# The end of a token mixer in another order: turned heads in the queries' place, the second tile's up products ahead of the first tile's, merging on VectorE, places of their own for the forget units

## What is computed

```python
def token_mixers(h, layer, ...):
    proj = h @ w_in                       # queries, keys, values of 3 branches, forget logits, gate logits
    dq, dk, dv, sq, sk, sv, fq, fk, fv, f_logit, g_logit = split(proj)
    o_diff = diff_attention(rope(dq), rope(dk), dv, lam)        # 4 heads, two score maps each
    o_diff = rms_norm(o_diff, diff_norm_g) * (1.0 - lam_init)
    o_sb = stick_breaking_attention(sq, sk, sv)                 # 4 heads
    o_fox = forgetting_attention(fq, fk, fv, log_sigmoid(f_logit + b_forget))   # scores + F_t - F_s
    gates = sigmoid(g_logit.reshape(B, S, 3, D))
    merged = (gates[:, :, 0] * (o_diff @ w_up_diff)
              + gates[:, :, 1] * (o_sb @ w_up_sb)
              + gates[:, :, 2] * (o_fox @ w_up_fox))
    return merged @ w_out
```

## Time and profile before

| | us |
|---|---|
| median of 3 runs | 1640.66 (1640.36 to 1644.25) |
| the profiled execution, its own time | 1641.09 |
| its span, first to last instruction | 1639.3 |
| TensorE busy | 1543.1 (94%) |
| VectorE busy | 959.9 (59%) |
| ScalarE busy | 743.1 (45%) |
| GpSimd busy | 40.5 (2%) |
| mean granted TensorE clock, 1 is full speed | 0.969 |

### The profile page before, as it was taken

The page is one execution under the profiler, slowest core; times in us unless marked ns, Lnnn a source line. Parts: engine busy times, 40 slices in busy tenths (PEclk is TensorE's granted clock), DMA queues, the critical chain, the costliest instruction groups (busy, mean ns, idle before and its releaser), DMA issues.

```text
span 1639.3 us, 18611 instructions
## 1 busy us (share of the span) xinstructions
PE 1543.1 (94%) x7572; PEld 1138.8 (69%) x7572; DVE 959.9 (59%) x883; ACT 743.1 (45%) x687; POOL 40.5 (2%) x30
## 2 busy tenths in 40 slices
PE   5999988999998998988999999999999999999995
PEld 4977766788886886867888536885368853688632
DVE  5547566555556637656799306993169931699413
ACT  3356653434432446653577205772057720577201
POOL 0000031000000000022000000000000000000000
PEclk9998989999999998988899999999999999999998
DMA  8353244454553352245999999999999999999994
GB/s 313 115 206 116 90 171 148 187 188 180 186 199 129 129 202 107 91 164 201 389 359 370 365 425 425 425 425 424 425 425 425 425 425 425 425 425 425 398 425 186
DMA packets 67013, 473.79 MB, mean 289 GB/s; under 512 B 8064, under 2 KB 8192, under 8 KB 10096
## 3 DMA queue, kind: packets, MB, share of 16 engines
q1 hardware_dynamic: 66096, 467.98, 70.8%
q0 software_dynamic: 832, 4.63, 0.8%
HBM read 471.53 MB, written 1.05 MB: 288 GB/s over the span
## 4 chain that ended last, share of the span: by engine, by line
PE 81%; DVE 10%; ACT 4%; issue 2%; DMA 2%; POOL 1%; SPq 0%; DVEq 0%; ACTq 0%
PE ps L1583 20%; PE ps L1584 19%; PE ps L1585 19%; PE ps L1929 11%; PE ps L1963 5%; PE ps L1889 2%; DVE lo_a L1026 2%; DMA raw_a<-in_w_item 1%; PE ps L1936 1%; ACT w_hi L698 1%; PE ps L1749 1%; PE ps L1613 1%; ACT w_hi L936 1%; DVE lo_b L1369 1%; DMA raw_a<-in_w_mix 1%
## 5 line engine op out<-in xcount | busy, mean ns | idle before, releaser
L1026 DVE TENSOR_TENSOR lo_a<-raw_a,w_hi 128x2048 fp32r<-128x2048 f32 (+2 forms) x117 | 251.2, 2151 | 198.7 <-ACT w_hi L698 197.7
L698 ACT ACTIVATE w_hi<-raw_a 128x2048 fp32r<-128x2048 f32 (+2 forms) x117 | 209.4, 1796 | 179.1 <-PE ps L1585 173.9
L1583 PE MATMUL ps<-w_hi,act_hi 128*128 128x512 f32 (+1 forms) x640 | 255.1, 399 | 26.3 <-DVE act_lo L1092 10.9
L1584 PE MATMUL ps<-lo_a,act_hi 128*128 128x512 f32 (+1 forms) x640 | 250.2, 391 | 0.0
L1585 PE MATMUL ps<-w_hi,act_lo 128*128 128x512 f32 (+1 forms) x640 | 249.8, 390 | 0.0
L1369 DVE TENSOR_TENSOR lo_b<-raw_b,w_hi 128x2048 fp32r<-128x2048 f32 x84 | 191.1, 2288 | 18.4 <-ACT w_hi L936 18.2
L936 ACT ACTIVATE w_hi<-raw_b 128x2048 fp32r<-128x2048 f32 x84 | 161.2, 1924 | 61.5 <-PE ps L1585 61.5
L1583 PE MATMUL ps<-w_hi,x_hi 128*128 128x512 f32 x448 | 176.6, 394 | 5.4 <-DVE lo_b L1369 3.2
L1585 PE MATMUL ps<-w_hi,x_lo 128*128 128x512 f32 x448 | 174.6, 390 | 0.0
L1369 DVE TENSOR_TENSOR lo_a<-raw_a,w_hi 128x2048 fp32r<-128x2048 f32 x71 | 161.5, 2289 | 18.1 <-ACT w_hi L936 17.9
L1583 PEld LDWEIGHTS ps<-w_hi,act_hi 128*128 128x128 f32 x640 | 125.8, 197 | 55.4 <-DVE lo_a L1026 8.4
(11 more groups left out here) (257 smaller groups left out, 2132.7 us busy)
## 6 DMA issues: line engine op xcount, KB each, us to landing
raw_a<-in_w_item SPq DMA_DIRECT2D x189, 1024.0 KB, 12.8
raw_b<-in_w_item SPq DMA_DIRECT2D x168, 1024.0 KB, 17.3
raw_a<-in_w_mix SPq DMA_DIRECT2D x60, 1024.0 KB, 4.8
raw_w<-in_w_item SPq DMA_DIRECT2D x21, 1024.0 KB, 16.4
raw_a<-in_w_mix SPq DMA_DIRECT2D x8, 512.0 KB, 3.5
ln_gb<-in_ln_mix POOLq DMA_DIRECT2D x2, 1024.0 KB, 5.1
cst<-in_consts SPq DMA_DIRECT2D x1, 1206.0 KB, 19.6
h<-in_x SPq DMA_DIRECT2D x2, 512.0 KB, 7.6
```

The source lines that it names most:

```text
L698: nc.scalar.activation(w_hi[:, HI_SLOT[g], 0:n], raw(slot)[:, 0:n], ACT.Copy).then_inc(s_hi, 1)
L1026: nc.vector.tensor_tensor(w_lo(slot)[:, 0:n], raw(slot)[:, 0:n], w_hi[:, HI_SLOT[g], 0:n].bitcast(F32), ALU.subtract).then_inc(s_lo, 1)
L1583: nc.tensor.matmul(dst, xh, wh, start=start, stop=False)
L1584: nc.tensor.matmul(dst, xh, wl, start=False, stop=False)
```

## The change

- `F_PART`, `f_hi`, `w_upper`: the upper halves of the two forget units lie in small places of their own. The ring of four holds only full units, so a unit's predecessor in its place (`HI_BEFORE`) is another one.
- `scores`: two heads' score matmuls one after the other, then their two forget products.
- `gates_copy` ahead of `exps` in the two `sb` groups, on ScalarE.
- The turned heads are split into `hd_hi` and `hd_lo`, in the queries' and keys' place, and the merged columns into `act_hi` and `act_lo`.
- Gate unit (5, 0), heads 3, the transposes of tile 1 and the turned weights of groups 4 and 5 come before gate unit (5, 1); the root mean square of group 3 starts before that unit.
- Column half 0 of the up products goes by tiles: tile 1 of all three branches, then tile 0.
- The third branch is added on VectorE, after the gating of a column half; the lower halves of the merged left columns come after all of column half 1.

```diff
-HEADS_JOB = [(1, 0, 4), (1, 1, 5), (0, 0, 2), (0, 1, 3)]
+HEADS_JOB = [(1, 0, 4), (1, 1, 5), (0, 0, 2), (0, 1, 4)]
...
-HI_SLOT = {_g: _q % HRING if _g < MOE_BASE else (_q - MOE_BASE + MOE_BASE % HRING) % MOE_HRING
-           for _q, _g in enumerate(SPLIT_UNITS)}
-HI_BEFORE = {_g: ([x for x in SPLIT_UNITS[:_q] if HI_SLOT[x] == HI_SLOT[_g]] or [None])[-1]
-             for _q, _g in enumerate(SPLIT_UNITS)}
+F_PART = {_b + U_F + _hk: _hk for _b in MIX_BASE for _hk in range(2)}
+FULL_UNITS = [g for g in SPLIT_UNITS if g not in F_PART]
+FULL_MIX = MOE_BASE - len(F_PART)
+HI_SLOT = {_g: _q % HRING if _g < MOE_BASE else (_q - FULL_MIX + FULL_MIX % HRING) % MOE_HRING
+           for _q, _g in enumerate(FULL_UNITS)}
+HI_BEFORE = {_g: ([x for x in FULL_UNITS[:_q] if HI_SLOT[x] == HI_SLOT[_g]] or [None])[-1]
+             for _q, _g in enumerate(FULL_UNITS)}
+for _g, _hk in F_PART.items():
+    HI_BEFORE[_g] = ([x for x in F_PART if x < _g and F_PART[x] == _hk] or [None])[-1]
...
+        f_hi = place("f_hi", [P, 2, 4 * NF], F32R)
...
-        mrg_hi = at("mrg_hi", [P, KT, SEQ], F32R, qkT_at)
-        mrg_lo = at("mrg_lo", [P, KT, SEQ], F32R, qkT_at + KT * SEQ * 4)
+
+        hd_hi = at("hd_hi", [P, KT, SEQ], F32R, qkT_at)
+        hd_lo = at("hd_lo", [P, KT, SEQ], F32R, qkT_at + KT * SEQ * 4)
...
+        def w_upper(g):
+
+            return f_hi[:, F_PART[g], :] if g in F_PART else w_hi[:, HI_SLOT[g], :]
...
 # GpSimd
                     pool.wait_ge(s_gm, l * 6 + (3 * cc + 2))
                     for t in range(TILES):
                         nc.gpsimd.tensor_tensor(cat[:, t, 512 * cc:512 * cc + 512], part(t, 0), part(t, 1), ALU.add).then_inc(s_pch, 1)
-
-                    pool.wait_ge(s_gm, l * 6 + (3 * cc + 3))
-                    pool.wait_ge(s_pch, l * 4 + (2 * cc + 2))
-                    for t in range(TILES):
-                        m = cat[:, t, 512 * cc:512 * cc + 512]
-                        nc.gpsimd.tensor_tensor(m, m, part(t, 2), ALU.add).then_inc(s_mrg, 1)
...
 # ScalarE, mixer
-                for g in range(1, 6):
+                for g in range(1, 5):
                     exps_first(g)
                     split(nb + U_GATE + 2 * g + 3, words(U_GATE + 2 * g + 3))
                     if g >= 2:
                         heads_copy(g - 2)
-                    exps(g)
-                    gates_copy(g)
+                    if GROUPS[g][0] == "sb":
+                        gates_copy(g)
+                        exps(g)
+                    else:
+                        exps(g)
+                        gates_copy(g)
                     split(nb + U_GATE + 2 * g + 4, words(U_GATE + 2 * g + 4))
                     turned_copy(g - 1)
-                    if g in (2, 5):
+                    if g == 2:
                         root(4)
-                transposed_hi(l * 4 + 1, act_hi, (0, 1), HEADS_JOB)
+
+                split(nb + U_UP + 1, words(U_UP + 1))
+                exps(5)
+                heads_copy(3)
+                transposed_hi(l * 4 + 1, hd_hi, (0, 1), HEADS_JOB)
+                turned_copy(4)
                 turned_copy(5)
+                root(4)
+                split(nb + U_UP + 2, words(U_UP + 2))
+                gates_copy(5)
                 heads_copy(4)
-                transposed_hi(l * 4 + 1, act_hi, (2,), HEADS_JOB)
                 heads_copy(5)
-                transposed_hi(l * 4 + 1, act_hi, (3,), HEADS_JOB)
+                transposed_hi(l * 4 + 1, hd_hi, (2, 3), HEADS_JOB)
                 for cc in range(2):
+                    split(nb + U_UP + 3 + cc, words(U_UP + 3 + cc))
                     for t in range(TILES):
                         part = gates[:, t, :, 512 * cc:512 * cc + 512]
                         nc.scalar.activation(part, part, ACT.Sigmoid).then_inc(s_sg, 1)
 
-                for k in range(U_UP, U_OUT + 2 + ahead):
+                for k in range(U_UP + 2, U_OUT + 2 + ahead):
                     split(nb + k + 3, words(k + 3))
                     if k == U_UP + 4:
-                        transposed_hi(l * 4 + 2, mrg_hi, (0, 1), MERGED_JOB)
+                        transposed_hi(l * 4 + 2, act_hi, (0, 1), MERGED_JOB)
                     if k == U_OUT:
-                        transposed_hi(l * 4 + 2, mrg_hi, (2, 3), MERGED_JOB)
+                        transposed_hi(l * 4 + 2, act_hi, (2, 3), MERGED_JOB)
...
 # VectorE, mixer
-                def rms(g):
+                def rms(g, meanwhile=None):
...
+                    if meanwhile:
+                        meanwhile()
                     refine(4, rn[:, 0:4])
...
-                for g in range(1, 6):
+                for g in range(1, 5):
                     group_first(g)
                     split(nb + U_GATE + 2 * g + 3, words(U_GATE + 2 * g + 3))
                     group_last(g)
                     split(nb + U_GATE + 2 * g + 4, words(U_GATE + 2 * g + 4))
-                    if g in (2, 5):
-                        rms(g - 2)
-                transposed_lo(l * 4 + 1, act_hi, act_lo, range(4), HEADS_JOB)
+                    if g == 2:
+                        rms(0)
+                group_first(5)
+                split(nb + U_UP + 1, words(U_UP + 1))
+                group_last(5)
+                rms(3, lambda: transposed_lo(l * 4 + 1, hd_hi, hd_lo, (0, 1), HEADS_JOB))
+                split(nb + U_UP + 2, words(U_UP + 2))
+                transposed_lo(l * 4 + 1, hd_hi, hd_lo, (2, 3), HEADS_JOB)
                 for cc in range(2):
                     for b in range(3):
                         k = U_UP + 3 * cc + b
...
                         ins.then_inc(s_gm, 1)
-                        if k == U_UP + 4:
-                            transposed_lo(l * 4 + 2, mrg_hi, mrg_lo, (0, 1), MERGED_JOB)
+
+                    dve.wait_ge(s_gm, l * 6 + (3 * cc + 3))
+                    for t in range(TILES):
+                        dve.wait_ge(s_pch, l * 4 + (2 * cc + t + 1))
+                        m = cat[:, t, 512 * cc:512 * cc + 512]
+                        nc.vector.tensor_tensor(m, m, gates[:, t, 2, 512 * cc:512 * cc + 512], ALU.add).then_inc(s_mrg, 1)
+                    if cc == 1:
+                        transposed_lo(l * 4 + 2, act_hi, act_lo, (0, 1), MERGED_JOB)
                 split(nb + U_OUT + 3)
-                transposed_lo(l * 4 + 2, mrg_hi, mrg_lo, (2, 3), MERGED_JOB)
+                transposed_lo(l * 4 + 2, act_hi, act_lo, (2, 3), MERGED_JOB)
...
 # TensorE, mixer
-                    for j in range(m):
-                        blk, r = j // 2, HD * (j % 2)
+
+                    def dst(j):
                         pos = place_of(g, j)
                         o = pos % (m // 2) * keys
-                        dst = z[:, pos // (m // 2), o:o + keys]
-                        k = qkT[r:r + HD, K_BLK[kind] + blk, 0:keys]
-                        ins = nc.tensor.matmul(dst, q, k, start=True, stop=kind != "fox")
+                        return z[:, pos // (m // 2), o:o + keys]
+
+                    for blk in range(m // 2):
+
+                        for j in (2 * blk, 2 * blk + 1):
+                            r = HD * (j % 2)
+                            q = qkT[r:r + HD, Q_BLK[kind] + blk, t * P:t * P + P]
+                            k = qkT[r:r + HD, K_BLK[kind] + blk, 0:keys]
+                            ins = nc.tensor.matmul(dst(j), q, k, start=True, stop=kind != "fox")
                         if kind == "fox":
-
-                            a = COLS["negsel"][0] + j * P
-                            ins = nc.tensor.matmul(dst, cst[0:NF, a:a + P], f_row[:, 0:keys], start=False, stop=True)
+                            for j in (2 * blk, 2 * blk + 1):
+                                a = COLS["negsel"][0] + j * P
+                                ins = nc.tensor.matmul(dst(j), cst[0:NF, a:a + P], f_row[:, 0:keys], start=False, stop=True)
                     ins.then_inc(s_sc, 1)
 
                 def turn_weights(g):
...
+                pe.wait_ge(s_gl, l * 6 + 5)
+                gate_unit(5, 0)
+                heads(3)
                 transposes(wait_tile1, cat, (0, 1), HEADS_JOB)
+                turn_weights(4)
                 turn_weights(5)
+                gate_unit(5, 1)
                 heads(4)
+                heads(5)
                 transposes(wait_diff0, cat, (2,), HEADS_JOB)
-                heads(5)
-                transposes(lambda t, half: pe.wait_ge(s_pve, l * 6 + 6), cat, (3,), HEADS_JOB)
+
+                def up_wait(cc, b):
+                    pe.wait_ge(s_lo, SPLIT_INDEX[nb + U_UP + 3 * cc + b] + 1)
+
+                def up_tile(cc, b, t):
+                    k0, n = ((0, 4), (4, 2), (6, 2))[b]
+                    return unit_tile(nb + U_UP + 3 * cc + b, t, 2 * b + t, range(k0, k0 + n), 512, hd_hi, hd_lo, True, True)
+
+
+                pe.wait_ge(s_tpl, l * 16 + 6)
+                pe.wait_ge(s_gl, l * 6 + 6)
+                for b in range(3):
+                    up_wait(0, b)
+                    up_tile(0, b, 1)
```

(29 more changed lines are left out.)

7 lines of the change are left out of this document (3 added, 4 removed).

## The result

| | median us | runs | ratio to before (95%) |
|---|---|---|---|
| before | 1641.34 | 1640.36 to 1644.25 | |
| changed | 1615.03 | 1611.31 to 1616.42 | 0.9834 (0.9822 to 0.9845) |

The account below looks back on a forecast made before the run. Expert-weight DMA sets the pace from 920 us but hangs on layer 1's mixer end. Gains of 14.1 and 13.6 us, less 1.0 per layer for the clock, gave -25.7 from 1641.09; median 0.4 lower, 1615.0; range 1606 to 1626.

Parts of the forecast that it names:

- Marks: Start of the output's second column half: 236.4 against 250.50 in layer 0 (-14.1), 739.9 against 753.55 in layer 1 (-13.6).
- Forget places: Ahead of the first gate unit: splits start earlier and TensorE loses its 1.75 us wait, sum -1.8 us.
- Fox pairs: Scores of group 2: sixteen pieces in 3.5 us instead of 5.77, -2.3; group 5 another -0.9.
- Gate copy: Copy moves into ScalarE's idle time; group 2's first gate unit at 130.6, group 0's heads at 138.3, -7.4 (layer 1 -8.2).
- The allowed fall of the clock: Possible at group 2's second gate unit or gate unit (5,1), 1.8 us each; 1.0 per layer allowed.
- Around the turned heads: Wait of 1.4 us for group 5's weights at 187.0, root mean square covered (3.91 before), up products from 195.2.
- The new wait: Ahead of the first output unit, TensorE waits 9.6 us (218.4 to 228.0) for lower halves queued on VectorE.
- Slow products behind it: First output half's 24 products run at a fallen clock: 5.5 us plus 2.0, ten products 0.2 longer.
- Rival 2: End of the mixer: VectorE keeps up, wait 4.0 instead of 9.6 us, 5.6 per layer more gained: 1604; chance 0.10.
- rival 3: Front gives less: pairs save nothing, clock falls in both places, or heads' copy later: 1619 to 1627; chance 0.18.
- rival 4: Nothing arrives at the end, because the expert part's loads run at their own pace: 1640.7; chance 0.05.
- rival 5: Slower: the long new wait leaves the low clock standing, all 96 output products slow: 1648; chance 0.05.

Follow-up runs that it names:

- front alone: Kernel before with only the forget units' own places, fox scores by pairs and gate copy ahead of the exponential, mixer's end as it was: 1619.82 us.
- Filling the wait: Changed kernel with 72 unused transposes of a constant matrix on TensorE in the wait ahead of the first output unit: 1609.73 us.
- the best kernel: Changed kernel with VectorE's column half 1 reordered: split, gatings 0 and 1, lower halves of left columns, gating 2, split, merging, split: 1591.58 us.
- the early lower halves: Changed kernel with the lower halves of the merged left columns made behind the second gating of column half 1: 1599.25 us.

## Why the prediction was right

That 1615.0 met 1615.03 is partly luck, but the working held at nearly every mark:

- **Marks.** The second output half comes 14.2 us earlier in layer 0 (forecast 14.1), and 29.45 in layer 1 (27.7). The first number hides an offset: in this execution everything from the kernel's first products on is 0.8 us later than in before (the forget units begin at 97.01 for 96.20), ahead of all that the change touches. Counted from there, layer 0 gives 15.0 (forecast 14.1), layer 1 by itself 14.3 (13.6), and 0.9 came between the mixers, where the forecast had nothing; 30 products are slow there in before and 20 now. By medians it is 26.3 against a forecast of 25.7, by the stretch 30.3: the 3.5 us between the medians and the traces had no place in the sum, and without them it would have been some 4 us short. That is the luck in it.
- **Forget places**: counted in the same way the first gate unit comes 1.9 us earlier, forecast 1.8 (the timelines alone say 1.08). In the front alone, where the offset is 0.1, the timelines themselves show 1.8. Taking them back costs 4.6 us over both layers, where 1.8 per layer is 3.6.
- **Fox pairs**: 3.38 us for sixteen against my 3.5. The direction was right (2.4 for eight forget pieces, measured 2.12), the score pieces 1.26 against 1.1. Only part of the old 5.77 was the order: with the pairs undone the sixteen take 5.25, the last of them at a falling clock, and 5.0 at 0.31 each.
- **Gate copy**: no wait for it is left, and the heads come at 139.07 for 138.3, the offset and nothing more, after a wait of 0.59 for the turned weights' copy, as "what is late next" had it. Group 2's first gate unit started at 132.77, 2.2 later than the 130.6 of the sum; that wait took it up (it is 2.12 in the front alone). The allowed fall of the clock came, but at group 1's second gate unit (115.86), not at group 2's.
- **Around the turned heads**: the wait for the weights of group 5 was 1.42 at 187.67 (forecast 1.4 at 187.0). The root mean square was covered, and up products began at 195.76 (195.2). With the pairs or the gate copy undone that wait is absent in both layers: it is slack that appears when TensorE is early.
- **The new wait**: 8.38 and 8.36 us, forecast 9.6, from 219.7 to 228.09 against 218.4 to 228.0. The end of VectorE's queue was right to 0.1 us on this clock, the offset of 0.8 included. The up products end 1.3 later than I had: they started 0.6 later and took 23.9 us where I had 23.2.
- **Slow products behind it**: nine and ten, 2.0 us each time, as forecast. Filling the wait gives 5.3 us back by the medians, 4 of them expected; the runs of that kernel lie 6.7 us apart.

**The sum's main wrong reading** is the front's share. I gave the front about 8 us per layer and the end 6, as if they were apart. Front alone gave 22.2 us, not 16.5, though its heads came when I had them, at 138.36 for 138.3. The 2.99 us stop in the earlier trace rows is put down to VectorE's gating there, and I booked it to the end alone. It is GpSimd's, its length depends on how the two engines' work falls together, and the earlier front wins most of it by itself; so does the new end. A smaller one: a low stretch covers 3 to 10 products in the mixer's waits of before (six from 238.63, three from 741.78) and 13 once, not 7 to 13.

Rival 2 (1604) was right about what is possible, not about this order: with VectorE's queue in another order the wait is 0.41 us. Against rival 3 the pieces took 3.38 us and the heads came within 0.8 us of the forecast. Against rival 4 stand the 885 us behind the mark, the same in both traces. Against rival 5: behind the 8.4 us stops come nine and ten slow products, in no mixer here more than fourteen.

## What the runs showed of the hardware

**GpSimd beside VectorE.** Two adds of 128x512 take 2.5 us when VectorE does nothing that counts, and what counts is the split (`lo_a<-raw_a,w_hi`, two inputs in SBUF). Worked out from the timelines of before, of the front alone and of the best kernel:

| two adds, us | beside splits, us | beside gatings and lower halves of merged columns, us |
|---|---|---|
| 5.59 | 3.33 | 2.1 |
| 4.56 | 2.40 | 1.5 |
| 4.42 | 2.08 | 0 |
| 2.56 | 0.54, at its end | 1.0 |
| 2.60 | 0.36, at its end | 2.4 |

In the first three rows a microsecond beside a split comes to 0.86 to 0.93 lost (over 2.5 us). But it is no price by the microsecond, as the single instructions in all twelve traces show. An add that starts with a split under way ends 1.12 to 1.18 us behind the end of the split, where it takes 1.25 to 1.34 alone. A split of a full unit that starts with an add under way ends 2.15 us behind the end of the add, for overlaps from 0.25 to 1.04 us, where it takes 2.28 alone: 2.68 us long in the fourth row, 2.51 in the last. So whichever starts second waits nearly all of the other's time, and in the last two rows VectorE paid. Work of VectorE that reads one input from PSUM costs nothing that can be seen, as the last row shows. The Trainium skill (GPSIMD Engine Reference, 1. Specifications) names contention with VectorE instructions that have two SBUF inputs, and these rows agree.

The prediction had a 0.6 us wait at the second merging by the rows, and none by the rule. Instead 1.0 us was lost at the first merging, which has two inputs in SBUF as well and starts just behind GpSimd's second add:

```profile
224.39 1.29 POOL L680 TENSOR_TENSOR cat<-gates 128x512 f32<-128x512 f32 x1
224.53 1.70 DVE L1282 TENSOR_TENSOR cat<-cat,gates 128x512 f32<-128x512 f32 x1
```

It takes 1.70 us instead of 0.69. The adds were that late because the first of them, from 221.15 on, met the split that starts at 220.99. So rule and rows agree here too; I had applied the rule to the gating alone.

**The clock.** Slow stretches of up to 14 products move between kernels that differ elsewhere: at 115.86 in the changed kernel, at 131.83 with the early lower halves, at 312.97 in before. Not every stop has one behind it: none follows the 1.75 us ahead of the first gate unit in the earlier trace rows. What decides where they fall is not settled by these runs. Shown is one case: with transposes up to the wait's end, the products behind it stayed at the upper level in both layers.

## What to carry to other kernels

When work is brought forward on the bounding engine, write down the queue of the engine that feeds it, instruction by instruction, and place the item that is waited for first. Here a wait of 8.4 us per layer could be read from that list beforehand, and a new order on VectorE alone gave 23 us, nearly as much as the whole change. Before a stop is put down to the engine that the profile names, look whether another engine's result ends just ahead of it. And what parts give by themselves must not be added where they shorten the same stop: 22.2 and 13.0 us made 26.3. Last, look at where the traces start to differ before you compare times in them: here 0.8 us of offset lay ahead of all that was changed.
